# 48 transposes of the identity on TensorE ahead of the first product of a four-layer transformer kernel

## What is computed

```python
h = rms_norm(x, attn_norm_g[l])
proj = h @ w_in[l]                      # 256 x 1024 times 1024 x 3584
rq, rk, rv, rg, dq, dk, dv = jnp.split(proj, split_at, axis=-1)
```

## Time and profile before

| what | value |
|---|---|
| median of three runs | 1545.16 us |
| the three runs | 1544.83, 1545.16, 1546.24 us |
| the profiled execution, its own time | 1547.99 us |
| span in its profile | 1546.1 us |
| PE busy | 1474.5 us (95%) |
| PE weight loads busy | 1217.8 us (79%) |
| DVE busy | 935.8 us (61%) |
| ACT busy | 795.7 us (51%) |
| POOL busy | 175.6 us (11%) |

### The profile page before, as it was taken

How to read it: one execution, slowest core, us unless ns; L and a number is a source line. 1 busy time by engine, 2 the same in 40 slices (tenths; PEclk the granted TensorE clock), 3 DMA queues, 4 the chain that set the end, 5 groups by cost and what they waited for, 6 DMA issues and landing times.

```text
span 1546.1 us, 21399 instructions
## 1 busy us (share of the span) xinstructions
PE 1474.5 (95%) x6967; PEld 1217.8 (79%) x6967; DVE 935.8 (61%) x1038; ACT 795.7 (51%) x970; POOL 175.6 (11%) x156
## 2 busy tenths in 40 slices
PE   5898899999897999999999999999999999999997
PEld 4777688888685788888878888888778788888885
DVE  4684555454674655544677886654546788766544
ACT  5474445445473555435566555453356765455442
POOL 0645000000555000000040000000002200000000
PEclk9998899999998999999999999999999999999999
DMA  7442465465442555466354575546553445655551
GB/s 287 150 136 83 139 195 192 167 204 166 136 137 82 164 190 168 147 229 181 110 172 151 166 236 189 176 150 224 187 184 111 159 145 181 233 191 165 189 164 41
DMA packets 157672, 258.03 MB, mean 167 GB/s; under 512 B 8633, under 2 KB 59011, under 8 KB 157443
## 3 DMA queue, kind: packets, MB, share of 16 engines
q1 hardware_dynamic: 154048, 249.95, 49.1%
q10 hardware_dynamic: 3523, 6.84, 1.4%
HBM read 255.71 MB, written 1.05 MB: 166 GB/s over the span
## 4 chain that ended last, share of the span: by engine, by line
PE 47%; issue 42%; POOL 5%; DVE 3%; ACT 1%; DMA 1%; POOLq 0%; ACTq 0%; DVEq 0%
PE bank L479 14%; PE bank L481 14%; PE bank L480 14%; PE bank L498 3%; POOL stat L2016 2%; POOL decay L2042 1%; DVE w_lo L1414 1%; PE bank L578 1%; POOL junk L2040 1%; ACT w_hi L947 1%; DMA crows<-in_conv_rows 1%; POOL proj L2050 0%; PE bank L746 0%; POOL cst L2106 0%; POOL proj L2082 0%
## 5 line engine op out<-in xcount | busy, mean ns | idle before, releaser
L1414 DVE TENSOR_TENSOR w_lo<-w_raw,w_hi 128x2048 fp32r<-128x2048 f32 (+1 forms) x251 | 554.9, 2218 | 226.2 <-ACT w_hi L947 223.3
L947 ACT CAST w_hi<-w_raw 128x2048 fp32r<-128x2048 f32 (+1 forms) x251 | 455.3, 1825 | 218.7 <-PE bank L481 213.1
L479 PE MATMUL bank<-w_hi,hT_hi 128*128 128x512 f32 (+1 forms) x1376 | 551.1, 401 | 13.9 <-DVE hT_lo L1439 6.3
L481 PE MATMUL bank<-w_hi,hT_lo 128*128 128x512 f32 (+1 forms) x1376 | 540.5, 393 | 0.0
L480 PE MATMUL bank<-w_lo,hT_hi 128*128 128x512 f32 (+1 forms) x1376 | 539.9, 392 | 0.0
L479 PEld LDWEIGHTS bank<-w_hi,hT_hi 128*128 128x128 f32 x1376 | 262.0, 190 | 71.8 <-issue 14.9
L481 PEld LDWEIGHTS bank<-w_hi,hT_lo 128*128 128x128 f32 x1376 | 261.4, 190 | 55.4
L480 PEld LDWEIGHTS bank<-w_lo,hT_hi 128*128 128x128 f32 x1376 | 262.3, 191 | 50.6
L2016 POOL TENSOR_TENSOR stat<-stat,cst 128x2 f32<-128x2 f32 (+3 forms) x23 | 41.0, 1782 | 1108.1 <-DVE stat L1463 967.9
L479 PE MATMUL bank<-w_hi,hid2T_hi 128*128 128x512 f32 x256 | 100.2, 392 | 0.0
L481 PE MATMUL bank<-w_hi,hid2T_lo 128*128 128x512 f32 x256 | 99.7, 390 | 0.0
(11 more groups left out here) (245 smaller groups left out, 1428.1 us busy)
## 6 DMA issues: line engine op xcount, KB each, us to landing
w_raw<-in_w_gate SPq DMA_DIRECT2D x108, 512.0 KB, 4.0
w_raw<-in_w_up SPq DMA_DIRECT2D x108, 512.0 KB, 4.6
w_raw<-in_w_down SPq DMA_DIRECT2D x104, 512.0 KB, 4.5
w_raw<-in_w_in SPq DMA_DIRECT2D x88, 512.0 KB, 4.4
w_raw<-in_w_out SPq DMA_DIRECT2D x16, 512.0 KB, 4.2
w_raw<-in_w_branch SPq DMA_DIRECT2D x32, 256.0 KB, 2.9
w_raw<-in_w_o SPq DMA_DIRECT2D x16, 512.0 KB, 4.6
bgate<-in_b_gate ACTq DMA_DIRECT2D x16, 256.0 KB, 3.3
```

Source lines behind the costliest of these rows:

```text
L479: pe.matmul(o, hi[:, kt, rows_of(r)], w_hi[:, s, j, 0:cols], start=begin, stop=False)
L481: mm = pe.matmul(o, lo[:, kt, rows_of(r)], w_hi[:, s, j, 0:cols], start=False, stop=end)
L947: act.copy(w_hi[:, s, 0:kts, :], w_raw[:, s, 0:kts, :]).then_inc(hi_ready, 1)
L1414: dve.tensor_tensor(w_lo[:, s, 0:kts, :], w_raw[:, s, 0:kts, :], w_hi[:, s, 0:kts, :].bitcast(F32), ALU.subtract).then_inc(lo_ready, 1)
```

## The change

One constant is added, and one loop on PE, behind the wait for the second half of x and ahead of the loop over the blocks. The loop transposes the identity 48 times into the first 128 columns of bank 6. Nothing reads the result. No other engine's program is changed.

```diff
@@ -37,6 +37,7 @@
 RING = 4
 AHEAD = 3
 LINE = 512
+WARM = 48
 
@@ -565,6 +566,9 @@
             turn_x(0)
             pe.wait_ge(x_rest_in, 16)
 
+            for _ in range(WARM):
+                pe.transpose(score[0][:, 0:P], ident, ident)
+
             for l in q.rounds(DEPTH, dict(slab=len(KTS1), blk=BLOCKS1, turn=TURNS1, scores=16, pool=2, dve=7)):
                 projection = [q.now("blk") + n for n in range(len(COLS1) + 1)]
```

## The result

The changed kernel is slower: median 1551.04 us over nine runs (1547.36 to 1552.16) against 1546.18 for the kernel before, now also over nine (1544.83 to 1547.52). Ratio 1.0025, 95% interval 1.0016 to 1.0034, that is +3.9 us (+2.5 to +5.3). A second measurement of the same kernel gave 1551.00 and 1.0024 (1.0014 to 1.0034). Forecast were 1543.6 and a range up to 1548.2, counted from the 1545.16 of the first three runs.

The account below looks back on a forecast made before the run. PE's work plus its own holes bound the kernel. First product 0.8 us later, twelve products 2.4 us shorter: -1.6 us from the median 1545.16 gives 1543.6 us, range 1541.6 to 1548.2.

Parts of the forecast that it names:

- The added code: On PE, 96 more instructions to fetch: cost nothing; nearest row if a fetch stalled, 0.17 us wait on issue.
- my four: Rivals: transposes don't raise the clock (0.08); gain doesn't carry (0.10); early rise, lucky restarts (0.06); clock falls again (nothing).
- Rival 1: Before PE's first product: transposes do not raise the clock, all 48 run slow, +4.6 us, 1549.7; chance 0.08.
- The wait on the second half of x: At PE's start: this load, landing at 13.85, sets the first added transpose at 13.9 us.
- A transpose costs 0.213 and 0.108: On PE: us per added transpose at the low and the high clock; all 48 take 10.2 or 5.2 us.
- The clock rises during the transposes: In PE's early hole: rise at 16.5 us (14.9 to 19.6), leaving 12 transposes slow and 36 fast.
- First product at 20.4 (19.6 to 21.9), second transposes of x at 23.2: PE's first stage: product 0.8 us later, twelve products 2.4 us shorter, sum -1.6; second transposes before at 24.82.
- The carry: From PE's first stage to the end: the 1.6 us gain carries whole, transposes of proj at about 59.0, not 60.59.
- Rival 2: Before 60.59: a hand-over to ACT, DVE or POOL takes the gain back, time 1545.2; chance 0.10.
- The scatter of later restarts: Later on PE: clock drops and rises met elsewhere, plus or minus 1 us for their sum.
- A gain of 2.4 and 1 us of luck: Early clock rise plus lucky later restarts: 1541.9 or less as a rival, chance 0.06; 1541.6 as the range's low end.
- the four cases: Own case 0.76; transposes don't raise the clock 0.08; gain doesn't carry 0.10; early rise and lucky restarts 0.06.

Follow-up runs that it names:

- pad16: The changed kernel with 16 semaphore increments more in PE's early hole; 1545.93 us, again 1546.08, ratio 0.9994 both times against the kernel before.

## Why the prediction was wrong

The step that failed is one sentence: "The added code (96 instructions to fetch) I cost at nothing; if a fetch did stall, the nearest row is PE's wait on issue in this stage, 0.17 us". It looked for the price of code at the place where the code was added. The price is paid at a loop head 1100 us behind, because adding code moves every later instruction against the fetch blocks. It is 3.4 to 3.7 us of gap and 1.4 to 1.8 of low clock, 4.8 to 5.5 together. No row shows such a stall, as the kernel before has none at that head; but the queue of kind "instruction" on its page and the branch in the program were there to be seen. The range should have had a rival "a boundary falls behind a loop head" with +5 us; none of my four was it. Rival 1 gave about the right number (1549.7) with the wrong mechanism, which is luck.

The other steps, point by point:

- *The wait on the second half of x.* Said 13.9 for the first transpose; 14.03, and 13.97 to 14.17 in the four traces with 48 transposes there.
- *A transpose costs 0.213 and 0.108.* 0.212 and 0.108.
- *The clock rises during the transposes,* at 16.5 (14.9 to 19.6). By the spacing, 18.3, 15.7, 16.6 and 18.0 in the four traces with 48 transposes, and from 15.4 to 18.6 in the six others whose transposes start at about 14. The rule that transpose mode doesn't release the clock (the Trainium skill, "TensorE: Matmul & The Clock Gate", Part 4) failed here a second time: nothing but transposes ran from 11.48 to 18.27. Rival 1 falls.
- *First product at 20.4 (19.6 to 21.9), second transposes of x at 23.2.* The same four traces (the changed kernel twice, pad16 twice): 21.29, 20.07, 20.42, 21.22, and 24.13, 22.92, 23.26, 24.05, against 24.82 before. Mean gain 1.2 us, 1.6 forecast; the late rise of the first trace is worth the 0.9 it lacks.
- *The carry.* Right as far as it can be followed: the transposes of proj start at 59.90, 58.68, 59.02 and 59.85 in those four traces against 60.59, which is 0.7, 1.9, 1.6 and 0.7 earlier, the same as at the second transposes of x. Rival 2 isn't needed. To the end it is not shown: pad16, the change without its stall, is at 0.9994 (0.9986 to 1.0003), twice, which is -0.9 us but not clear of zero.
- *The scatter of later restarts*, put at 1 us. Too small for one execution: the profiled one was 5.1 us ahead at 1116 from 0.7 at the start.
- *Small slips.* The earlier trace rows has a second slice at 7 tenths, the last one. A gain of 2.4 and 1 us of luck from 1545.16 make 1541.8, not 1541.6 or 1541.9. The chances of the four cases already add up to 1.00, so no rest was left for noise. None of this bears on the result.

So the sum should have been -1.2 of the start plus 4.8 to 5.5 of the stall, +3.6 to +4.3; measured were +3.9 by the ratio and +4.9 by the medians.

## What to carry to other kernels

Code in front of a loop isn't always free even where its time is hidden: it moves the loop's head against the blocks in which code is fetched. In a long loop whose code is fetched anew on each pass, look for a wait on "issue" a few instructions behind its head, and if there is one, move the head with a few fillers where the engine is idle anyway, or change the count of what you add; here 16 instructions were worth 5 us, more than the change itself could win. When an effect is a few us, test the changed size at both sides (40, 48, 56) before you believe in its mechanism: of the five sizes tried (20, 32, 40, 48, 56) only 48 was slower than the kernel before.

## What the runs showed of the hardware

- A short loop inside a layer shows no such transfer while it turns: in the kernel before no transfer of 16 KB of the instruction queue q8 starts between 199.2 and 318.6 us, where five passes are made over one and the same code, and PE is busy throughout.
- A semaphore increment of its own costs PE's queue 0.151 us (24.2 for 160), more than a transpose with its weight load at the high clock (0.108).
- Work of nothing but transposes of f32 lets TensorE's clock rise from 1.2 to 2.4 GHz, here at 15.7 to 18.3 us in four traces; PE had done transposes from 11.5 on, with one gap of some 0.4 us.
- After a branch back to the head of the second layer, the second transfer of 16 KB on the instruction queue landed 6.1 to 6.8 us after the first began (14 traces); six times PE stood still, and went on 1.3 to 1.5 us after it had landed.
- The clock fell to 0.50 in or just behind the gaps of 3.0 to 3.7 us (four traces); at those of 1.6 and 0.8 us, one trace each, it did not.
